# One-hot matrices of the expert gates: j built alone, i and its gate parts with the token innermost

## The reference, cut to what matters

```python
s1, i1 = lax.top_k(s[:, :, 0], PEER_TOPK)
s2, i2 = lax.top_k(s[:, :, 1], PEER_TOPK)
cand_i = i1[..., :, None] * PEER_NKEYS + i2[..., None, :]
top_s, pos = lax.top_k(cand_s, PEER_TOPK)
eidx = jnp.take_along_axis(cand_i, pos, axis=-1)
gate = jax.nn.softmax(top_s, axis=-1)
h = jax.nn.gelu(jnp.einsum('thkd,td->thk', u[eidx], xb), approximate=False)
return jnp.einsum('thk,thkd->td', gate * h, v[eidx])
```

## Time and profile before

| | |
|---|---|
| median of 3 runs | 3046.05 us (3037.42 to 3047.87) |
| the profiled execution, its own time | 3046.59 us |
| its span, first to last instruction | 3044.8 us |
| TensorE busy | 2601.4 us (85%) |
| VectorE busy | 2260.7 us (74%) |
| ScalarE busy | 874.0 us (29%) |
| GpSimd busy | 267.6 us (9%) |
| granted TensorE clock, mean | 0.90 |
| first PEER layer: u pass, of it with gate groups | 342 to 776 us, 492 to 762 us |
| second PEER layer: u pass, of it with gate groups | 1390 to 1825 us, 1540 to 1810 us |

### The profile page before, as it was taken

How to read it: one execution, slowest core, us unless ns; L and a number is a source line. 1 busy time by engine, 2 the same in 40 slices (tenths; PEclk the granted TensorE clock), 3 DMA queues, 4 the chain that set the end, 5 groups by cost and what they waited for, 6 DMA issues and landing times.

```text
span 3044.8 us, 42055 instructions
## 1 busy us (share of the span) xinstructions
PE 2601.4 (85%) x16904; PEld 2325.3 (76%) x16904; DVE 2260.7 (74%) x3118; ACT 874.0 (29%) x1285; POOL 267.6 (9%) x100
## 2 busy tenths in 40 slices
PE   6977999999999987579999999999685673676888
PEld 6856998999888866379999998888584472555886
DVE  6767798999666676378889986666675636675786
ACT  1000344444555531004444444555212001000000
POOL 0000493000000000007910000000000000000000
PEclk8988999999999998589999999999895555787899
DMA  5524576666777763046766567777541000341454
GB/s 190 179 70 148 178 214 185 187 184 188 246 256 242 242 197 114 0 136 183 209 185 187 182 204 256 243 241 243 155 136 38 0 15 0 116 136 59 129 167 137
DMA packets 201473, 485.52 MB, mean 159 GB/s; under 512 B 23296, under 2 KB 93312, under 8 KB 200768
## 3 DMA queue, kind: packets, MB, share of 16 engines
q1 hardware_dynamic: 194784, 467.75, 49.8%
q10 hardware_dynamic: 6496, 15.09, 1.5%
HBM read 448.15 MB, written 34.60 MB: 159 GB/s over the span
## 4 chain that ended last, share of the span: by engine, by line
PE 58%; DVE 32%; POOL 4%; DMA 3%; issue 2%; ACT 1%; ACTq 0%; DVEq 0%
PE psum L845 23%; PE psum L649 21%; DVE halves L1920 7%; DVE rounded L1229 7%; PE psum L798 6%; DVE halves L1917 5%; POOL rounded L617 4%; PE psum L1018 2%; DVE rounded L1225 2%; DMA sb<-in_u_turned 1%; PE psum L687 1%; DVE rounded L1299 1%; DVE sb L1663 1%; PE psum L921 1%; PE psum L919 1%
## 5 line engine op out<-in xcount | busy, mean ns | idle before, releaser
L1229 DVE TENSOR_TENSOR rounded<-sb,rounded 128x1024 fp32r<-128x1024 f32 (+3 forms) x696 | 813.9, 1172 | 243.3 <-ACT rounded L2133 233.7
L649 PE MATMUL psum<-rounded 128*128 128x256 f32 (+1 forms) x4380 | 734.0, 332 | 96.0 <-DVE rounded L1299 43.9
L649 PEld LDWEIGHTS psum<-rounded 128*128 128x128 f32 x4380 | 661.8, 200 | 168.4 <-DVE rounded L1299 47.9
L798 PE MATMUL psum<-rounded 128*128 128x256 f32 x6144 | 775.2, 285 | 13.3 <-POOL rounded L617 13.2
L2133 ACT ACTIVATE rounded<-sb 128x1024 fp32r<-128x1024 f32 x512 | 542.8, 1060 | 789.9 <-PE psum L798 342.4
L798 PEld LDWEIGHTS psum<-rounded 128*128 128x128 f32 x6144 | 748.7, 192 | 16.3 <-POOL rounded L617 16.3
L845 PE MATMUL psum<-rounded,weights 128*128 128x512 f32 x3072 | 697.3, 389 | 0.4 <-ACT sb L2149 0.4
L845 PEld LDWEIGHTS psum<-rounded,weights 128*128 128x128 f32 x3072 | 576.3, 188 | 120.7 <-issue 1.2
L617 POOL TENSOR_TENSOR rounded<-sb,rounded 128x1024 fp32r<-128x1024 f32 x96 | 267.4, 2803 | 1264.6 <-ACT rounded L2133 1263.7
L1225 DVE CAST rounded<-sb 128x1024 fp32r<-128x1024 f32 (+4 forms) x289 | 181.3, 627 | 195.8 <-PE psum L649 173.1
L1920 DVE TENSOR_TENSOR halves<-halves,small 128x1536 bf16<-128x1536 bf16 x128 | 225.0, 1758 | 4.4
(11 more groups left out here) (281 smaller groups left out, 1377.5 us busy)
## 6 DMA issues: line engine op xcount, KB each, us to landing
sb<-in_u_turned SPq DMA_DIRECT2D x256, 512.0 KB, 3.8
sb<-in_peer_v SPq DMA_DIRECT2D x256, 512.0 KB, 3.7
hidden<-sb SPq DMA_DIRECT2D x256, 128.0 KB, 3.8
sb<-hidden SPq DMA_DIRECT2D x256, 128.0 KB, 3.6
sb<-in_ret_w_in SPq DMA_DIRECT2D x48, 512.0 KB, 4.4
sb<-in_ffn_w_up SPq DMA_DIRECT2D x40, 512.0 KB, 4.1
sb<-in_peer_w_q SPq DMA_DIRECT2D x32, 512.0 KB, 4.1
sb<-in_ffn_w_down SPq DMA_DIRECT2D x22, 512.0 KB, 4.0
```

What stands on the lines that cost most here:

```text
L649: mm = pe.matmul(o, a[p], b[q], start=(first and i == 0), stop=(last and i == 2), skip_group_check=True)
L798: mm = pe.matmul(ps(bank, 1)[:, 0:T], u[p][:, k * P:(k + 1) * P], hT[:, q, k, :], start=(k == 0 and w == 0), stop=(k == KD - 1 and w == 2))
L1229: vec.tensor_tensor(ring_lo[0:k, part, 0:wide], ring[0:k, slot, 0:wide], ring_hi[0:k, part, 0:wide].bitcast(F32), ALU.subtract).then_inc(c ...
```

## The change

The one-hot of j becomes an instruction of its own with 512 elements, laid out as before (token, then the number 0 to 127 innermost). The one-hot of i becomes another of 512 elements, laid out with the four tokens innermost, and is compared with a new table `iota_four` that holds every number four times. The three gate parts follow the layout of i: 1536 elements as before, tokens innermost. The matmuls then read the moving operand with a step of four bf16 elements (8 bytes); the stationary operand is read as before. The table is made once for each PEER layer, in the free scratch.

```diff
+        misc_at = lasting.at
         misc = lasting.take(512)
...
-        ij_onehot = half_parts.take(2, 2, 4, P)
-        gate_onehot = half_parts.take(2, 3, 4, P)
+        i_onehot, j_onehot = half_parts.take(2, P, 4), half_parts.take(2, 4, P)
+        gate_onehot = half_parts.take(2, 3, P, 4)
...
+        iota_four = nc.alloc_sbuf_tensor_at("iota_four", [P, P, 4], BF16, offset=SB_AT + 4 * misc_at + 16)
...
-                            mm = pe.matmul(ps(4 + buf, 1)[:, q * P:(q + 1) * P], ij_onehot[:, buf, 1, q, :],
-                                           gate_onehot[:, buf, p, q, :], start=(q == 0 and p == 0), stop=(p == 2),
+                            mm = pe.matmul(ps(4 + buf, 1)[:, q * P:(q + 1) * P], j_onehot[:, buf, q, :],
+                                           gate_onehot[:, buf, p, :, q], start=(q == 0 and p == 0), stop=(p == 2),
                                            skip_group_check=True)
...
                 vec.tensor_copy(iota_half, iota).then_inc(*own.next())
+                vec.tensor_copy(iota_four[:, :, :], bcast(iota, 2, 4)).then_inc(*own.next())
...
-                    vec.tensor_tensor(ij_onehot[:, buf], bcast(bcast(iota_half, 1, 4), 1, 2), bcast(routes[:, 0:2, t], 3, P),
+                    vec.tensor_tensor(j_onehot[:, buf], bcast(iota_half, 1, 4), bcast(routes[:, 1, t], 2, P),
                                       ALU.is_equal).then_inc(*own.next())
-                    done()
-                    vec.tensor_tensor(gate_onehot[:, buf], bcast(ij_onehot[:, buf, 0], 1, 3), bcast(routes[:, 2:5, t], 3, P),
+                    vec.tensor_tensor(i_onehot[:, buf], iota_four[:, :, :], bcast(routes[:, 0, t], 1, P),
+                                      ALU.is_equal).then_inc(*own.next())
+                    done()
+                    vec.tensor_tensor(gate_onehot[:, buf], bcast(i_onehot[:, buf], 1, 3), bcast(routes[:, 2:5, t], 2, P),
                                       ALU.mult).then_inc(*own.mark(onehots_made))
```

## The result

| | before | changed |
|---|---|---|
| median, 4 runs each | 3041.74 us (3037.25 to 3047.87) | 3115.36 us (3108.62 to 3117.08) |
| ratio | 1 | 1.0237 (95% interval 1.0209 to 1.0264) |
| profiled execution | 3046.59 us | 3108.62 us |
| VectorE busy | 2260.7 us | 2144.2 us |

(A fourth run of the kernel before has joined the three in the table ahead of the change; the median moved from 3046.05 to 3041.74 us by it.) VectorE did the 116 us less work that was asked of it, and the kernel became slower. The 3030 us of the forecast was wrong; the first rival, TensorE slowed by the step of its moving operand, was put at 3110.

What follows compares the result with a forecast made beforehand. VectorE was taken as the bound, TensorE close behind; 7.6 us of pace plus 1.0 us of first wait per layer, 17.2 for both, took 3046.6 to 3029.4, stated as 3030 us. Range 3026 to 3113, the forecast's own 3026 to 3036.

Steps and rivals of the forecast that it cites:

- the first rival: Group matmuls: the moving operand's 8-byte step slows TensorE, 0.63 us x 128 groups = 80 us, total 3110 us; chance 0.34.
- what bounded the kernel: Tiles 47 to 122 of each u pass: VectorE sets the pace, 21.43 us per period against TensorE's 20.94.
- the prices of VectorE's instructions: One-hots after the change: j 0.69 us, i 0.42, gates 0.96; group 1.93 us start to start, from 2.93.
- the cap that TensorE sets on the gain: First to last group: TensorE needs 262.1 us against 269.69 measured, so 7.6 us to be had per layer.
- The first wait: TensorE's wait for the first group's one-hots in each layer: falls to 1.35 us, 1.0 us saved.
- The slow tile: Tile 48, 4.46 us in place of 2.96: counted as gone, 1.5 us per layer; if left in both, 3032.4 us.
- the one on the matmuls: The 12 matmuls per group, moving operand stepping 8 bytes per column: claimed no added cost, 54 ns each as before.
- The other bound that stood beside it: Same matmuls: all bytes stepped over fetched at 9.6 bytes per ns, 106 ns a matmul, 0.63 us more per group.
- The other rivals: VectorE stays at one element per cycle, 3056 us, chance 0.07; another wait eats half the gain, 3038 to 3044, chance 0.08.

## Why the prediction was wrong

**Right:** what bounded the kernel (VectorE by 0.5 us in 21.45), the prices of VectorE's instructions, two elements at a time included (958 and 419 ns against 0.96 and 0.42 us), the cap that TensorE sets on the gain, and the size of that gain, 17 us forecast and 18 us in the run with adjacent reads. The first wait fell from 2.35 to 1.35 us as worked out. The slow tile behind that wait, at a lower clock, went away in the first layer. In the second, where the wait was 1.58 us, one tile still took 1572.66 - 1568.21 = 4.45 us, so "I count the slow tile as gone" was half right:

```profile
1566.91 1.55 PE L823 MATMUL psum<-halves 128*128 128x128 bf16 x12 [1.58 <-DVE halves L1925]
1568.21 4.61 PE L800 MATMUL psum<-rounded 128*128 128x256 f32 x24
1572.66 1.55 PE L823 MATMUL psum<-halves 128*128 128x128 bf16 x12
```

The first run with two tokens innermost had the same wait of 1.58 us there and no slow tile (2.96 us), so the length of the wait alone does not decide it.

**The step that failed** is the one on the matmuls: "I take nothing, since no row shows a byte limit, only a column rate". The other bound that stood beside it, 106 ns, 0.63 us more a group, 3110 us, is what came: 108 ns, 0.65 us more, 3108.6 us in the profiled execution. That the total comes so close is partly luck: the groups cost 2 to 3 us more than that bound and the slow tile of the second layer 1.5 us, while latent attention happened to take 5.7 us less. The median, 3115.36 us, lies above even the 3113 that was to take in this rival. The choice between the ends was made as if the trace were neutral, and the nearest rows were not: float32 matmuls have four columns in 16 bytes, the change has two, and nothing ran at full rate with fewer than four. To take the same 54 ns was to extend the column rate past everything that had been seen of it.

The wrong part of the rival was its form. It priced the bytes stepped over, 9.6 per ns; the experiments show lines of 16 bytes, one per 1.64 ns, which has the same price up to a step of 16 bytes and then stops growing (210 ns at 16 and at 24 bytes). At the 8 bytes of the change the two forms agree, so the wrong one gave nearly the right price.

The Trainium skill was cited on both sides. Its SBUF — State Buffer, Specifications (TRN2), asks for at least two accesses to each 16-byte line; the runs bear the line out, but for TensorE's moving operand two columns per line give half the rate (108 ns against 54), and at four it is 57 ns. The Trainium skill's Vector Engine (DVE) Microarchitecture Reference, 5.2, with 1.73 ns for a Vector port that hops with every element, gave an estimate of 111 ns and lay near TensorE's 1.64 ns per line; that both have one cause is not shown.

**The other rivals** did not come: VectorE reached two elements per cycle, and no other wait took the gain.

## What to carry to other kernels

A layout that helps the engine that writes an operand must be priced on the engine that reads it, above all when that one stands right behind as the next bound: here 1.0 us saved on VectorE was capped at 0.13 us per group, and 0.65 us were added to TensorE. For a moving operand keep at least four columns in every 16 bytes (adjacent float32, or bf16 with a step of two). If a step of four is needed for the writer, make that operand the stationary one, where it cost 1 to 2 ns a matmul. This was measured with bf16 operands of 128 columns; strided float32 reads and larger steps of the stationary operand were not.

## What the runs showed of the hardware that was not expected

**The clock fell without an idle engine.** With the steps of 16 and 24 bytes some tiles take 4.57 us start to start and others 3.08. The stretches of such a tile and of the slow reads after it, in the run with 24 bytes:

```profile
605.80:610.30 4.50, 4.50 (x26) 4.48 (x24) 2.02 (x4) 0.60 (x1) 0.00 (x0) 0.62 0.48 146
610.40:612.80 2.40, 2.40 (x12) 1.23 (x12) 1.11 (x1) 1.33 (x2) 0.00 (x0) 1.00 0.00 0
```

PE shows no idle time, yet the granted clock is 0.62 in the tile, a mixture of 1.2 and 2.4 GHz, right behind 2.5 us of matmuls that took a column only every 1.64 ns; during the next slow group it is back at 1.00. Not every tile behind a slow group is slow: in the first layer about 30 of the 50 tiles that stand alone between two groups are. From the first to the last group the run with 24 bytes takes 931.16 - 492.24 = 438.92 us in the first layer and 2146.49 - 1710.27 = 436.22 us in the second, and 63 steps of 2.52 + 2.96 us with 12 tiles of 2.89 would be 379.9. The difference is 115 us for both layers, so the 110 and 117 us by which the two runs exceed the sum by lines lie there, most of it in the slow tiles. What makes the clock fall was not tested apart. With the change's 8 bytes the clock stayed at 1.00 over the groups, but for one tile after the first wait of the second layer.
